# Two weight tiles side by side behind two normalizations, with filler matmuls moved into TensorE's idle times

## The chip, the cores and the metric

One core of a Trainium2 chip runs the whole program in one launch. The metric is the device time in microseconds (us), a median of several executions. The engines are named as in the profile: PE is TensorE (PEld its weight loads), DVE is VectorE, ACT is ScalarE, POOL is GpSimd, SP issues the DMAs.

## The reference

Two model blocks run one behind the other on one sequence of 1024 tokens with 1024 features, all in float32. Only the parts around the change are written out:

```python
# first block: two layers with an adaptive norm
for layer in range(2):
    shift, scale, gate = split(silu(c) @ ada_w[layer] + ada_b[layer], 3)
    h = rms_norm(x, norm_w[layer]) * (1 + scale) + shift
    y = even_mixer(h, ...) if layer % 2 == 0 else odd_mixer(h, ...)   # attention, gates, output projection
    x = x + gate * y
x = rms_norm(x, final_norm)

# odd_mixer: h @ w_in gives q (1024), k (256), v (256), gates (1024); windowed attention with a sink;
#            (attention * silu(gates)) @ w_out

# second block
h = rms_norm(x, norm1)
p = h @ w_in              # 512 lru_x, 512 lru_g, 256 q, 256 k, 512 v, 512 g, 16 z
lru = rg_lru(causal_conv(lru_x), ...) * gelu(lru_g)
gla = rms_norm(gated_linear_attention(q, k, v, z)) * silu(g)
x = x + concat(lru, gla) @ w_out
h = rms_norm(x, norm2)
gate, up = split(h @ w_ffn_in, 2)
x = x + (silu(gate) * up) @ w_ffn_out
return rms_norm(x, final_norm_2)
```

## The kernel before

**Layout.** Activations lie with features on the partitions: eight blocks of 128 features ("k" or "f") by 1024 tokens. A float32 product is made from a high part and a low part of each operand: the weight tile is `WH + WL`, the normalized activations are `HH + HL`, and a product is `HH*WH + HL*WH + HH*WL`.

**A weight tile.** Projections go through a list of tiles of 128 output features, numbered through the whole kernel. For tile `t`, SP loads the raw weights (`sp_weights`, it waits for `w_low` of tile `t - 2`), ACT rounds them to the high part (`act_high`, L241), POOL subtracts for the low part (`pool_low`, L246), PE makes 48 matmuls of 512 columns (`pe_tile`, L259: eight features of six matmuls each), and ACT or DVE takes the result out of PSUM (`act_evict`, L268, or `dve_residual`, L410). Tiles alternate between two places for the weights and two pairs of PSUM banks by `t % 2`. A tile can have places of its own (`own_places`); the first tile of each of the two output projections has them.

**A change of stage.** Between an output projection and the next projection stands the norm of `x`. ACT squares each feature block of the new `x` and DVE adds them up. PE sums over features with a column of ones (`pe_token_sums`, L348). ACT and DVE make the inverse root (L353, L358), DVE copies it out over 128 columns (`dve_spread`, L362), and PE turns it round into PSUM banks 6 and 7 (`pe_spread`, L368). Then the norm is applied feature by feature: DVE scales (L381), ACT adds the shift and rounds to `HH` (L392), DVE subtracts for `HL` (L386, which reads two operands in SBUF). The first tile of the projection is multiplied while this goes on: before its feature `k` PE waits for `n_low(n, k)`, which is `HL` of feature `k`. The second tile comes behind it in `pe_tile`'s order.

**Fillers.** `pe_stay_awake(n, bank)` (L343) issues `n` matmuls of 128 columns whose results nobody reads. Each gives two records in the profile.

**The three places.** `n = 1` is layer 1 of the first block: output projection `EVEN_OUT`, then the tiles `ODD_PROJ`. `n = 2` is the second block: output projection `ODD_OUT`, then `S_PROJ`. Here the spread is made twice: once for `final_norm` (it is copied to SBUF, L1863) and once, called "gained", for both norms in a row. `n = 3` is the norm before the feed-forward part, where DVE L2422 and L2433 and ACT L2428 take the place of L381, L386 and L392.

**Orders written by hand.** Each engine runs its own list of functions (`pe_...`, `act_...`), in program order. ACT makes the high part of tile `t + 1` before it takes out tile `t`. In `act_odd_proj` and `act_second_proj` the high part of the first tile comes before the normalization and that of the second tile behind it. SP issues all DMAs from one list: in `sp_odd_proj` the first tile's weights, then a 4 MB copy of `x` to memory (`spill`) that waits for the last residual, then the other tiles; in `sp_second_proj` the first tile's weights, then the recurrent weights `BD` and `WAL` that wait for DVE's memsets, then the others. `dve_conv(0)` needs tile 0 of `S_PROJ`; `pe_recurrent(0)`, behind feature 4 of tile 2, needs that convolution.

Of the kernel before, what the change touches and what calls it, by code (L numbers as in the profile page):

```python
# [14 lines left out]
P = 128  # L15
# [3 lines left out]
DT = DM // P  # L19
# [112 lines left out]
def build(nc, d, where, known):  # L132
# [71 lines left out]
    tiles = []  # L204
# [31 lines left out]
    def act_high(t):  # L236
        raw, high, _ = places(t)
        act.wait_ge(*w_loaded[t % 2].at(t))
        if t >= 2:
            act.wait_ge(*w_used.at(t - 2))  # L240
        act.activation(high[:, :, :], raw[:, :, :], ACT.Copy).then_inc(*w_high.up(t))  # L241
# [5 lines left out]

    def pe_tile(t, high, low, made=None, beside=None):
        s, w = t % 2, tiles[t]
        _, wh, wl = places(t)  # L250
        pe.wait_ge(*w_low.at(t))
        if t >= 2:
            pe.wait_ge(*evicted(t - 2))
        for k in range(w.kt):
            if made:
                pe.wait_ge(*made(k))
            for n, (wt, x) in enumerate(((wh, high), (wh, low), (wl, high))):
                for h in range(2):
                    last = pe.matmul(ps[0:w.m, 2 * s + h, :], wt[:, k, :], x[:, k, halves(h)],  # L259
                                     start=(k == 0 and n == 0), stop=(k == w.kt - 1 and n == 2))  # L260
            if k == w.kt - 1:
                last.then_inc(*w_used.up(t))
            if beside:
                beside(k)

    def act_evict(t, dst, func=ACT.Copy, scale=1.0):
# [31 lines left out]
    EVEN_OUT = [tile(cols(d["even_w_out"][0], i * P), gone="dve", own=None if i else EVEN_FIRST) for i in range(8)]  # L298
    ODD_KV = [tile(cols(odd_in, O_K + i * P)) for i in range(4)]
    ODD_Q = [tile(cols(odd_in, O_Q + i * P)) for i in range(8)]  # L300
    ODD_GATES = [tile(cols(odd_in, O_G + i * P)) for i in range(8)]
    ODD_OUT = [tile(cols(d["odd_w_out"][0], i * P), gone="dve", own=None if i else ODD_FIRST) for i in range(8)]
    S_LRU = [tile(cols(second_in, S_LX + i * P)) for i in range(4)]
    S_Z16 = tile(cols(second_in, S_Z + 16 - P))
# [5 lines left out]

    def act_tiles(ts, evict, first=False, upto=None):

        if first:
            act_high(ts[0])
        for i, t in enumerate(ts):
            if upto is None or t + 1 <= upto:
                act_high(t + 1)
            evict(i, t)

# [1022 lines left out]
    def pe_even_out():  # L1342
        pe.wait_ge(*e_done.at("B", N - 1))
        pe_stay_awake(14, 2 * (EVEN_OUT[0] % 2))
        for f, t in enumerate(EVEN_OUT):
            pe_tile(t, HH, HL, made=(lambda k: m_low.at(0, k)) if f == 0 else None)
        pe_stay_awake(12, 4)
        pe_token_sums(1, 4)
        pe_spread(1)
        pe_stay_awake(14, 0)  # L1350

# [39 lines left out]
    def sp_odd_proj():  # L1391
        sp_weights(ODD_PROJ[0])
        sp.wait_ge(*ev_dve.at(EVEN_OUT[-1]))
        sp.dma_start(d["spill"], X[:, :, :]).then_inc(*x_spilled.landed(1))
        for i, t in enumerate(ODD_PROJ[1:]):
            sp_weights(t)
            if i == 2:
                sp.dma_start(AWAY[:, :], const("away")).then_inc(*c_tables.landed(0))
                sp.dma_start(SLOPE[:, :], const("slopes")).then_inc(*c_tables.landed(1))
                sp.dma_start(SINK[:, :], d["c_sink"][0:1, :].to_broadcast([P, C_HEADS])).then_inc(*c_tables.landed(2))  # L1400

    def pe_odd_proj():
        for i, t in enumerate(ODD_PROJ):
            pe_tile(t, HH, HL, made=(lambda k: n_low.at(1, k)) if i == 0 else None)
            if 4 <= i < 6:
                f = i - 4
                pe.wait_ge(*ev_act.at(ODD_KV[2 + f]))
                for t in range(TT):
                    last = pe.transpose(pair(4 + 2 * f)[:, rows(t)], VFC[:, f, rows(t)], IDENT[:, :])
                last.then_inc(*vc_turned.up(f))  # L1410

    def act_odd_proj():
        act_high(ODD_PROJ[0])
        act_normalize(1, MOD[:, 24:32])
# [19 lines left out]

        act_tiles(ODD_PROJ, evict, upto=ODD_PROJ[-1])

# [372 lines left out]

    def pe_odd_out():  # L1810
        pe.wait_ge(*c_added.at(NG - 1))
        pe_stay_awake(15, 2 * (ODD_OUT[0] % 2))
        for f, t in enumerate(ODD_OUT):
# [87 lines left out]
    def sp_second_proj():  # L1901
        for j, t in enumerate(S_PROJ):
            sp_weights(t)
            if j == 0:
                sp.wait_ge(*bd_clear.at())
# [84 lines left out]
    def pe_second_proj():  # L1990
# [18 lines left out]

        for j, t in enumerate(S_PROJ):  # L2010
            pe_tile(t, HH, HL, made=(lambda k: n_low.at(2, k)) if j == 0 else None, beside=lambda k: beside(j, k))

# [56 lines left out]
    def act_second_proj():  # L2069
        act_high(S_PROJ[0])  # L2070
        act_normalize(2, None)
        for j, t in enumerate(S_PROJ):
            act_high(t + 1)
            if j in (3, 5, 7, 9):
# [198 lines left out]
    def pe_second_out():  # L2273
        for f, t in enumerate(S_OUT):
            pe_tile(t, HM, LM, made=(lambda k: m_low.at(2, k)) if f == 0 else None)
        pe_stay_awake(12, 4)
        pe_token_sums(3, 4, LAST.sq)
        pe_spread(3, LAST)
        pe_stay_awake(13, 0)
# [654 lines left out]
```

## Time and profile before

| | |
|---|---|
| median of 3 runs | 2529.44 us (2526.62 to 2530.26) |
| the profiled execution's own time | 2526.05 us |
| its span in the trace | 2524.7 us |
| mean granted clock of PE | 0.984 |
| PE busy | 2389.8 us, 95% |
| DVE, ACT, POOL busy | 1410.3, 1134.7, 918.5 us |

The granted clock is 1.00 at 2.4 GHz and 0.50 at 1.2 GHz. In the views of the trace, idle time stands in square brackets with what ended it; start times are from the span's start. Busy time is the union of an engine's records, so overlapping records count once.

### The profile page before, as it was taken

Reading aid. Unit: us, or ns where it says so; the run is one execution under the profiler, and the core shown is the slowest. Engines: PE = TensorE matmul, PEld = TensorE weight load, DVE = VectorE, ACT = ScalarE, POOL = GpSimd, SP = SyncE. Lnnn points to the kernel's source line nnn. Section 1 sums busy time; section 2 is a strip of 40 time slices with the busy share of each in tenths; the row PEclk is TensorE's granted clock in tenths of the full one; section 3 lists DMA queues with packets and bytes.
Section 4 is the critical chain, followed back from the end, with each engine's and each line's share of the span. In section 5 each row is a group of like instructions: output and inputs, shape, how many; then the busy total and the mean of one; then the engine's idle time right before and its main releaser. Section 6 shows DMA issues by size and latency. Waiting matters only on the chain.

```text
span 2524.7 us, 31336 instructions
## 1 busy us (share of the span) xinstructions
PE 2389.8 (95%) x12088; PEld 1955.3 (77%) x12088; DVE 1410.3 (56%) x1948; ACT 1134.7 (45%) x1753; POOL 918.5 (36%) x671
## 2 busy tenths in 40 slices
PE   4999999989999999999999999999989999999998
PEld 3778788868888778876678677788867888788876
DVE  5256499858884420149954743332556666665665
ACT  4322388778883221259942473231333333333334
POOL 0121234236642122335421211112265555566651
PEclk8999999999999999999999999999999999999999
DMA  8234300000003211100030411013201111111111
GB/s 293 73 117 135 106 6 1 1 18 1 1 1 117 100 54 49 43 1 1 10 117 22 133 34 42 26 29 113 67 26 51 50 51 50 51 50 51 50 57 69
DMA packets 152488, 143.23 MB, mean 57 GB/s; under 512 B 10358, under 2 KB 140692, under 8 KB 150420
## 3 DMA queue, kind: packets, MB, share of 16 engines
q1 hardware_dynamic: 152340, 141.22, 17.7%
q8 instruction: 97, 1.59, 0.3%
q14 instruction: 51, 0.42, 0.1%
HBM read 124.43 MB, written 16.78 MB: 56 GB/s over the span
## 4 chain that ended last, share of the span: by engine, by line
PE 66%; ACT 8%; DVE 8%; POOL 8%; issue 6%; DMA 4%; SPq 1%; ACTq 0%; DVEq 0%; POOLq 0%
PE ps L259 36%; PE ps L2509 6%; PE ps L1031 4%; POOL WSR L2398 4%; PE ps L2496 4%; PE ps L1054 3%; DMA WS<-in_w_ffn_in 3%; PE ps L1041 3%; POOL WSL L2416 2%; PE ps L2472 2%; ACT C_PR L1687 1%; DVE XF L2724 1%; POOL OWL L2640 1%; PE ps L1576 1%; ACT B_PR L1114 1%
## 5 line engine op out<-in xcount | busy, mean ns | idle before, releaser
L246 POOL TENSOR_TENSOR WL<-WR,WH 128x1024 fp32r<-128x1024 f32 (+1 forms) x91 | 211.3, 2322 | 909.5 <-ACT WH L241 909.4
L259 PE MATMUL ps<-HH,WH 128*128 128x512 f32 (+1 forms) x1168 | 374.8, 402 | 15.6 <-DVE HL L386 9.9
L259 PE MATMUL ps<-HL,WH 128*128 128x512 f32 (+1 forms) x1168 | 363.8, 393 | 0.0
L259 PE MATMUL ps<-HH,WL 128*128 128x512 f32 (+1 forms) x1168 | 363.0, 392 | 0.0
L259 PEld LDWEIGHTS ps<-HH,WH 128*128 128x128 f32 (+1 forms) x1168 | 214.7, 189 | 75.0 <-DVE HL L386 14.0
L259 PEld LDWEIGHTS ps<-HH,WL 128*128 128x128 f32 (+1 forms) x1168 | 220.1, 188 | 48.8
L259 PEld LDWEIGHTS ps<-HL,WH 128*128 128x128 f32 (+1 forms) x1168 | 219.8, 188 | 48.9
L2724 DVE TENSOR_TENSOR XF<-ps,XF 128x1024 f32<-128x1024 f32 x168 | 199.8, 1218 | 24.4 <-PE ps L2509 20.1
L2496 PE MATMUL ps<-HC,WSH 128*128 128x512 f32 x640 | 197.4, 390 | 4.8 <-DVE HC L2455 4.8
L2410 ACT ACTIVATE WSH<-WSR 128x512 fp32r<-128x512 f32 x100 | 63.2, 632 | 303.6 <-POOL WSR L2398 303.5
L2398 POOL TENSOR_TENSOR WSR<-WS 128x512 f32<-128x512 f32 x100 | 137.9, 1379 | 151.3 <-PE ps L2496 71.8
L1067 DVE TENSOR_REDUCE NM<-ps 128x1 f32<-128x1024 f32 x128 | 156.1, 1220 | 35.1 <-PE ps L1031 34.4
L2416 POOL TENSOR_TENSOR WSL<-WSR,WSH 128x512 fp32r<-128x512 f32 x100 | 135.3, 1353 | 79.1 <-ACT WSH L2410 79.1
L2496 PE MATMUL ps<-HS,WSH 128*128 128x512 f32 x480 | 149.1, 392 | 3.3 <-DVE HS L2455 3.3
L2496 PEld LDWEIGHTS ps<-HC,WSH 128*128 128x128 f32 x640 | 119.9, 188 | 30.8 <-DVE HC L2455 3.3
L2509 PE MATMUL ps<-AH,OWH 128*128 128x512 f32 x352 | 114.4, 406 | 11.0 <-DVE XF L2724 10.6
L2496 PE MATMUL ps<-HC,WSL 128*128 128x512 f32 x320 | 124.5, 389 | 0.0
L2684 DVE TENSOR_TENSOR CG<-CG,ps 128x512 f32<-128x512 f32 x60 | 41.3, 688 | 146.5 <-ACT CU L2570 94.0
L2509 PE MATMUL ps<-AH,OWL 128*128 128x512 f32 x352 | 109.9, 393 | 0.0
L2509 PE MATMUL ps<-AL,OWH 128*128 128x512 f32 x352 | 109.1, 391 | 0.0
L2496 PEld LDWEIGHTS ps<-HS,WSH 128*128 128x128 f32 x480 | 90.7, 189 | 22.9 <-issue 3.4
L1606 DVE CUSTOM_DVE_ANT_0 C_SB<-ps,BF,NSINK 128x384 f32<-128x384 f32 (+1 forms) x128 | 68.9, 576 | 69.4 <-POOL C_VS L1728 60.3
(411 smaller groups left out, 5160.7 us busy)
## 6 DMA issues: line engine op xcount, KB each, us to landing
WS<-in_w_ffn_in SPq DMA_DIRECT2D x44, 512.0 KB, 5.0
MKW<-in_ada_w SPq DMA_DIRECT2D x32, 512.0 KB, 4.2
spill<-X SPq DMA_DIRECT2D x3, 4096.0 KB, 13.2
OW<-in_w_ffn_out SPq DMA_DIRECT2D x22, 512.0 KB, 3.4
WR<-in_w_in SPq DMA_DIRECT2D x21, 512.0 KB, 3.7
WR<-in_odd_w_in SPq DMA_DIRECT2D x20, 512.0 KB, 3.6
WR<-in_even_w_in SPq DMA_DIRECT2D x17, 512.0 KB, 4.9
AWK<-in_ada_w SPq DMA_DIRECT2D x8, 1024.0 KB, 10.1
```

Source lines behind the costliest of these rows:

```text
L246: pool.tensor_tensor(low[:, :, :], raw[:, :, :], high[:, :, :].bitcast(F32), ALU.subtract).then_inc(*w_low.up(t))
L259: last = pe.matmul(ps[0:w.m, 2 * s + h, :], wt[:, k, :], x[:, k, halves(h)], start=(k == 0 and n == 0), stop=(k == w.kt - 1 and n == 2))
L1031: last = pe.matmul(ps[:, b + j, :], qs[:, rows(q)], ks[:, halves(j)], start=(n == 0), stop=(n == len(passes) - 1))
L1041: last = pe.transpose(ps[:, 4 + j, rows(k)], D.PR[:, p % 3, rows(4 * j + k)], IDENT[:, :])
L1054: last = pe.matmul(ps[:, 6 + pg % 2, 0:2 * P], D.VS[D.v_of(h)][:, k, :], pt[pg % 2][:, k, :], start=(k == 0 and n == 0), stop=(k == TT - 1 ...
L1067: dve.tensor_reduce(NM[:, s % 4:s % 4 + 1], pair(2 * (s % 2)), AX_X, ALU.max, negate=True).then_inc(*m_done.up(g, s))
L1606: dve.tensor_tensor_reduce(C_SB[:, hd, WIN - w:WIN], ps[:, j, 0:w], BF[i % 2][:, hd, b0:b0 + w], -1.0, NSINK[:, 4 * i + hd:4 * i + hd + 1] ...
L2398: pool.tensor_tensor(WSR[:, q % RING, :, :], w_block(*a), w_block(*b), op).then_inc(*ws_sum.up(q))
L2416: pool.tensor_tensor(WSL[:, q % RING, :, :], src, WSH[:, q % RING, :, :].bitcast(F32), ALU.subtract).then_inc(*ws_low.up(q))
L2496: last = pe.matmul(ps[:, BANK[o], :], w[:, q % RING, k, :], OPERAND[o][:, x, k, :], start=(k == 0 and n == 0), stop=(k == HK - 1 and n == 2))
L2509: done = pe.matmul(ps[:, 4 + 2 * (n % 2) + h, :], w[:, rows(n)], x[:, halves(h)], start=(first and m == 0), stop=(last and m == 2))
L2724: dve.tensor_tensor(LAST.x[:, n, :], pair(4 + 2 * (n % 2)), LAST.x[:, n, :], ALU.add).then_inc(*y_added.up(r, n))
```

## The change

Both first tiles get their weights early and are multiplied in turn, feature by feature, for six features; then the first tile's last two features, then the second's. For that the first tile of each of the two projections has places of its own (`KEYS_FIRST`, `LRU_FIRST`), ACT makes both high parts before the normalization, SP issues three (layer 1) or two (second block) tiles' weights before the DMAs named above, and `act_high` waits for the last user of the shared place. The fillers are set differently at three stage changes: five more before the spreads `n = 1` and `n = 3` (and 13 in place of 14 behind the first of these); at the start of `ODD_OUT` seven stand before the wait for the attention's last result and nine behind it, where 15 stood behind it.

```diff
 def act_high(t):
+        user = t - 2
+        while user >= 0 and tiles[user].own:
+            user -= 2
         act.wait_ge(*w_loaded[t % 2].at(t))
-        if t >= 2:
-            act.wait_ge(*w_used.at(t - 2))
+        if user >= 0:
+            act.wait_ge(*w_used.at(user))

+    def pe_feature(t, k, high, low):        # the six matmuls of one feature, with pe_tile's waits at k == 0
+        ...
+    def pe_two_tiles(first, second, high, low, made):
+        for k in range(DT - 2):
+            pe.wait_ge(*made(k))
+            pe_feature(first, k, high, low)
+            pe_feature(second, k, high, low)
+        for t in (first, second):
+            for k in range(DT - 2, DT):
+                pe.wait_ge(*made(k))
+                pe_feature(t, k, high, low)

+    KEYS_FIRST, LRU_FIRST = own_places("KEYS_FIRST", 59, 63, 67), own_places("LRU_FIRST", 67.25, 71.25, 75.25)
-    ODD_KV = [tile(cols(odd_in, O_K + i * P)) for i in range(4)]
+    ODD_KV = [tile(cols(odd_in, O_K + i * P), own=None if i else KEYS_FIRST) for i in range(4)]
-    S_LRU = [tile(cols(second_in, S_LX + i * P)) for i in range(4)]
+    S_LRU = [tile(cols(second_in, S_LX + i * P), own=None if i else LRU_FIRST) for i in range(4)]

+    def act_two_tiles(first):
+        act_high(first)
+        act_high(first + 1)

 def pe_even_out():
         pe_token_sums(1, 4)
+        pe_stay_awake(5, 5)
         pe_spread(1)
-        pe_stay_awake(14, 0)
+        pe_stay_awake(13, 0)

 def sp_odd_proj():
-        sp_weights(ODD_PROJ[0])
+        for t in ODD_PROJ[:3]:
+            sp_weights(t)
         sp.wait_ge(*ev_dve.at(EVEN_OUT[-1]))
         sp.dma_start(d["spill"], X[:, :, :]).then_inc(*x_spilled.landed(1))
-        for i, t in enumerate(ODD_PROJ[1:]):
+        for i, t in enumerate(ODD_PROJ[3:]):
             sp_weights(t)
-            if i == 2:
+            if i == 0:
                 ...

 def pe_odd_proj():
+        pe_two_tiles(ODD_PROJ[0], ODD_PROJ[1], HH, HL, lambda k: n_low.at(1, k))
         for i, t in enumerate(ODD_PROJ):
-            pe_tile(t, HH, HL, made=(lambda k: n_low.at(1, k)) if i == 0 else None)
+            if i >= 2:
+                pe_tile(t, HH, HL)

 def act_odd_proj():
-        act_high(ODD_PROJ[0])
+        act_two_tiles(ODD_PROJ[0])
         act_normalize(1, MOD[:, 24:32])
         ...
-        act_tiles(ODD_PROJ, evict, upto=ODD_PROJ[-1])
+        act_high(ODD_PROJ[2])
+        evict(0, ODD_PROJ[0])
+        evict(1, ODD_PROJ[1])
+        for i, t in enumerate(ODD_PROJ):
+            if i >= 2:
+                if i + 1 < len(ODD_PROJ):
+                    act_high(t + 1)
+                evict(i, t)

 def pe_odd_out():
+        pe_stay_awake(7, 0)
         pe.wait_ge(*c_added.at(NG - 1))
-        pe_stay_awake(15, 2 * (ODD_OUT[0] % 2))
+        pe_stay_awake(9, 2 * (ODD_OUT[0] % 2))

 def sp_second_proj():
         for j, t in enumerate(S_PROJ):
             sp_weights(t)
-            if j == 0:
+            if j == 1:
                 sp.wait_ge(*bd_clear.at())

 def pe_second_proj():
-        for j, t in enumerate(S_PROJ):
-            pe_tile(t, HH, HL, made=(lambda k: n_low.at(2, k)) if j == 0 else None, beside=lambda k: beside(j, k))
+        pe_two_tiles(S_PROJ[0], S_PROJ[1], HH, HL, lambda k: n_low.at(2, k))
+        for j, t in enumerate(S_PROJ[2:], 2):
+            pe_tile(t, HH, HL, beside=lambda k: beside(j, k))

 def act_second_proj():
-        act_high(S_PROJ[0])
+        act_two_tiles(S_PROJ[0])
         act_normalize(2, None)
         for j, t in enumerate(S_PROJ):
-            act_high(t + 1)
+            if j == 0:
+                act_high(t + 2)
+            elif j > 1:
+                act_high(t + 1)

 def pe_second_out():
         pe_token_sums(3, 4, LAST.sq)
+        pe_stay_awake(5, 5)
         pe_spread(3, LAST)
```

## Rows read from the trace of the kernel before

**Rows 1.** Page, part 1: busy us, share, instructions by engine.
```profile
PE 2389.8 (95%) x12088; PEld 1955.3 (77%) x12088; DVE 1410.3 (56%) x1948; ACT 1134.7 (45%) x1753; POOL 918.5 (36%) x671
```

**Rows 2.** Waits of PE, whole span: us in total, times, longest.
```profile
PE ps L259 <- DVE HL L386: 9.9, 12, 0.9
PE ps L259 <- POOL WL L246: 7.2, 6, 1.9
```

**Rows 3.** Timeline, layer 1's first tiles: start, us, instructions, [idle before].
```profile
871.04 0.71 PE L259 MATMUL ps<-HH,WH 128*128 128x512 f32 x2
...
875.13 0.74 PE L259 MATMUL ps<-HH,WH 128*128 128x512 f32 x2 [0.86 <-DVE HL L386]
...
890.16 0.84 PE L259 MATMUL ps<-HH,WH 128*128 128x512 f32 x2 [1.94 <-POOL WL L246]
...
902.78 0.62 PE L259 MATMUL ps<-HH,WH 128*128 128x512 f32 x2
```

**Rows 4.** Windows: length, busy (records) of the five engines, PE clock, DMA, GB/s.
```profile
888.20:890.60 2.40, 0.46 (x3) 0.40 (x3) 2.33 (x3) 1.97 (x2) 2.20 (x2) 1.00 0.00 0
...
1275.00:1276.50 1.50, 0.00 (x0) 0.00 (x0) 0.83 (x2) 0.59 (x1) 0.00 (x0) 0.95 0.00 0
1276.50:1279.80 3.30, 3.26 (x15) 3.26 (x16) 1.32 (x2) 2.48 (x3) 0.72 (x1) 0.51 0.38 112
...
863.30:866.90 3.60, 2.65 (x13) 2.65 (x14) 1.50 (x3) 0.88 (x1) 2.36 (x1) 0.50 0.98 414
866.90:870.10 3.20, 3.20 (x17) 3.20 (x17) 3.14 (x4) 2.30 (x2) 0.00 (x0) 0.50 0.76 199
```

**Rows 5.** Timeline, stage change into layer 1.
```profile
860.84 1.95 PE L348 MATMUL ps<-ONEC,SQX 128*128 128x1 f32 x16 [1.05 <-DVE SQX L338]
...
864.25 1.97 PE L368 MATMUL ps<-IDENT,SQX 128*128 128x128 f32 x8 [1.47 <-DVE SQX L362]
864.26 2.36 POOL L246 TENSOR_TENSOR WL<-WR,WH 128x1024 fp32r<-128x1024 f32 x1 [22.98 <-ACT WH L241]
...
866.26 2.47 DVE L381 SCALAR_TENSOR_TENSOR T<-X,GS,ps 128x1024 f32<-128x1024 f32 x2 [2.06 <-PE ps L368]
...
868.76 1.28 DVE L386 SCALAR_TENSOR_TENSOR HL<-T,MOD,HH 128x1024 fp32r<-128x1024 f32 x1
```

**Rows 6.** Timeline, start of the output projection ODD_OUT.
```profile
1276.54 5.13 PE L343 MATMUL ps<-IDENT 128*128 128x128 f32 x30 [1.56 <-DVE C_O L1644]
...
1278.48 4.63 DVE L406 TENSOR_TENSOR HL<-MIX,HH 128x1024 fp32r<-128x1024 f32 x4 [1.99 <-ACT HH L401]
...
1281.43 0.70 PE L259 MATMUL ps<-HH,ODD_FIRST 128*128 128x512 f32 x2
```

**Rows 7.** Timeline, stage change into the second block and its first two tiles.
```profile
1376.78 2.48 PE L343 MATMUL ps<-IDENT 128*128 128x128 f32 x10
...
1379.47 2.36 POOL L246 TENSOR_TENSOR WL<-WR,WH 128x1024 fp32r<-128x1024 f32 x1 [25.40 <-ACT WH L241]
...
1382.52 0.69 DVE L362 COPY SQX<-RC 128x1024 f32<-128x1024 f32 x1
...
1384.15 2.98 PEld L343 LDWEIGHTS ps<-IDENT 128*128 128x128 f32 x26
...
1388.26 0.70 PE L259 MATMUL ps<-HH,WH 128*128 128x512 f32 x2 [0.94 <-DVE HL L386]
...
1406.32 0.73 PE L259 MATMUL ps<-HH,WH 128*128 128x512 f32 x2 [0.44 <-POOL WL L246]
...
1417.34 0.62 PE L259 MATMUL ps<-HH,WH 128*128 128x512 f32 x2
```

**Rows 8.** Timeline, DVE and POOL at the same time, second block.
```profile
1409.22 3.31 DVE L2137 SCALAR_TENSOR_TENSOR CV<-LX,COLB,CV 128x1024 f32<-128x1024 f32 x1
...
1407.97 3.47 POOL L246 TENSOR_TENSOR WL<-WR,WH 128x1024 fp32r<-128x1024 f32 x1 [1.70 <-ACT WH L241]
```

**Rows 9.** DVE's conv instructions, L2137: ns min/median/max.
```profile
L2137 DVE SCALAR_TENSOR_TENSOR CV<-LX,COLB,CV x12: 1283/1285/3306, 1407.9 to 1496.0; 128x1024 f32<-128x1024 f32 x12
```

**Rows 10.** Timeline, spread before the feed-forward part.
```profile
1796.22 1.97 PE L368 MATMUL ps<-IDENT,SQF 128*128 128x128 f32 x8 [1.47 <-DVE SQF L362]
```

**Rows 11.** Windows, late in the second projection.
```profile
1600.00:1620.00 20.00, 20.00 (x98) 16.87 (x98) 4.93 (x4) 4.85 (x5) 2.44 (x1) 0.74 0.10 27
```

## What the change will do, predicted before it was run

> **What bounds the kernel now.** I read the page first: PE is busy for 2389.8 of 2524.7 us [rows 1], so what can be won is the some 135 us in which it idles, and time in which it runs at half clock. The waits of PE come next. Of its waits inside the tiles' matmuls (L259), the two largest are 9.9 us for `HL` in 12 pieces and 7.2 us for `WL` in six [rows 2]. The timeline shows where they lie. In layer 1 the first tile starts at 871.04, and before a feature PE idles some 0.86 us [rows 3], because DVE delivers a feature each 2.5 us (two instructions of 1.24 to 1.28 us, [rows 5]) and six matmuls need less. Then the second tile waits 1.94 us for its low weights, since ACT made their high part only behind the normalization. Tile 2 starts at 902.78 [rows 3]. In the second block tile 0 starts at 1388.26, tile 1 at 1406.32, tile 2 at 1417.34 [rows 7]. The windows show the clock: 1.00 up to 890.6 with PE almost idle from 888.2 [rows 4]. The matmuls from 890.16 on then run partly at half clock: the tile takes 902.78 - 890.16 = 12.6 us, and the one at full clock in the second block 1417.34 - 1406.32 = 11.0 us.
>
> **Two tiles in turn, layer 1.** Removed: the waits per feature, the wait for `WL`, and the 1.6 us of half clock. A pair of features costs PE 2 x 11.0 / 8 = 2.75 us, more than DVE's 2.5, so after the first feature PE never waits: `HL` of feature 7 is there at most 7 x 2.51 = 17.6 us after that of feature 0, and PE asks for it behind 13 features' work, 17.9 us after its start. Both tiles take 22.0 us from PE's start. Switching tile and bank at each feature I cost at nothing: two tiles behind each other also switch and show no gap (902.78). Bounded from above by the 0.86 us of a real wait, 12 switches would cost 10 us; nothing speaks for it, as nothing is waited for.
>
> PE's start: five fillers now stand before the spread. The sums end at 862.8 and the spread began at 864.25 [rows 5]. Ten records take 2.48 us at half clock [rows 7] and some 1.2 us at full (26 records of the fillers from 1384.15 took 2.98, [rows 7]). The clock fell at 863.3 [rows 4], so they take about 2.0 us: the spread starts at 864.9, 0.6 later than now, and DVE behind it too. `HL` of feature 0 was ready at 868.76 + 1.28 = 870.04, and now at 870.7. In return PE has no gap in front of the spread. Where it was busy without a gap from the fall on, the clock was back after 3.3 us (1276.5 to 1279.8, [rows 4]); with the gap it was low up to 870.1 [rows 4]. So it should be back at 866.7, 13 fillers take 3.1 us, and PE starts at 870.7 with `HL`, against 871.04. Were the clock low to 870.1 after all, it would start at 871.7. Tile 2 then starts at 870.7 + 22.0 = 892.7: **10.1 us won**, between 9.1 and 10.4.
>
> What could be late next. POOL makes the second low part at 866.6 to 869.0, directly behind the first (2.36 us from 864.26, [rows 5]), and DVE's first L386 comes at 869.4: no meeting. If they met, it would cost what is left of POOL's instruction, at most 2.4 us. Tile 2's high part comes behind the normalization (about 887.2), its low part is ready at 891, its banks are free at about 891, and PE comes at 892.7: cover of 1.7 us. The spill now waits behind the weights of tile 2, which wait for POOL at 866.6: about 8 us later; only the eviction of tile 4, 20 us behind 892.7, waits for it. ACT's second high part (1.04 us) lies in ACT's idle time before the first `T`. From tile 2 on all is paced by PE and moves forward as a whole.
>
> **Fillers at the start of ODD_OUT.** PE idles 1.5 us before 1276.5, the clock falls, and 30 filler records take 5.13 us, so the first tile starts at 1281.43 although its first `HL` is ready at 1278.48 + 1.16 = 1279.7 [rows 4, 6]. Seven fillers in the idle time (1.6 us at full clock) keep PE busy, and nine behind the wait take 2.1 us at full clock. The tile then starts at 1279.75: 1.7 us won. If the clock falls anyway, the nine take 4.4 us and 0.3 us is won. I take **1.6**.
>
> **Two tiles, second block.** By the same sum tile 2 would start at 1388.26 + 22.0 = 1410.3, against 1417.34: 7.1 us. But here the second low part meets something. POOL's first ran from 1379.47 to 1381.83 [rows 7], and now the second follows to 1384.2. DVE's copy for the spread "gained" started at 1382.52 and took 0.69 us [rows 7]; in front of it is a tiny instruction with two operands in SBUF. Such a meeting is in the trace: while POOL ran from 1407.97 to 1411.44, DVE's L2137 took 3.31 us [rows 8], where its kind takes 1.285 [rows 9]; it ended one normal length after POOL did. So both DVE instructions wait for 1384.2, and the copy ends near 1385.1 instead of 1383.2: 1.9 us on the path of the spread. By itself this costs between 0 (if a copy of one operand is not held) and 2.3 us. The Trainium skill (SBUF — State Buffer, "Who interferes with whom") says that VectorE and GpSimd share one port pair as an exclusive lock, that a copy in a 2-port mode and any VectorE instruction with two SBUF inputs need it, and that the later one waits for the whole instruction. By that rule the copy is held as I have it; the rows show it for two-input instructions, and here it speaks against making both weights early.
>
> PE meanwhile has nothing from 1382.6 to 1385.1, 2.5 us. A gap of 1.9 us was followed by half clock [rows 4], so I expect the clock to fall here. The spread (8 records, 1.97 us low against 1.0) and the 26 filler records (2.98 at full, some 6.4 all low) then end at 1391 to 1393.5; with no fall, `HL` at 1390.1 sets the start. I take 1391.4, 3.1 us later than before: **4.0 us won**, between 1.9 and 7.1. Downstream: conv(0) ends some 6 us after tile 0 and `pe_recurrent(0)` is asked for 6.8 us after tile 1, so it is covered.
>
> **Five fillers before the feed-forward part.** The spread began at 1796.22 after an idle 1.47 us [rows 10], the same pattern: 0.6 us later, clock earlier. Nothing lies behind it that gains. I take **0**, between 0.9 lost and 0.3 won.
>
> **Sum.** 10.1 + 1.6 + 4.0 + 0 = 15.7 us. The profiled execution took 2526.05 us (span 2524.7 and 1.35 around it) and would take 2510.4. It was 3.4 us quicker than the median of 2529.44. On the median: 2513.7.
>
> **Rivals.**
> - A, no price in the second block: the copy isn't held by POOL, or the clock stays up. Then the second block wins 5.3 to 7.1 us, for a sum of about 18 and 2511.4. For it: the L1863 copy next door reads PSUM and may be of the kind that isn't held. Against it: [rows 8].
> - B, the gain of the second block is used up: the low-clock fillers run to 1393.5 and a wait of DVE's chain (conv(0), then eight updates of X, then recurrence 0) reaches PE. Then only 11.7 us remain: 2517.7. Against it: DVE's end of the updates has some 3 us of cover before recurrence 0.
> - C, the other side: the clock. Late in the second projection PE was busy for all of 20 us at a mean clock of 0.74 [rows 11], so half of that stretch ran low and lost 5 us. Which stretches are caught changes when everything moves by 12 to 16 us. A microsecond at half clock loses half a microsecond, so 21 us more of it than now would eat 10.7 of the 15.7 us and leave less than 0.2% (5 us); 31 us would eat all. The likely size is 7 us either way (3.5 us of time), for a time of 2517 or 2510; 2525 or more needs three or four such stretches together.
> - D, the change doesn't do what it says: PE waits at each switch, up to 0.86 us a time; 24 switches lose 20 us, for 2534. Against it: nothing releases PE there.
>
> **How the numbers follow.** Chances: forecast 0.52, A 0.22, B 0.15, C at its deciding size 0.07, D 0.04. The bounds of the terms, all bad at once, give 9.1 + 0.3 + 1.9 - 0.9 = 10.4 us, and all good 10.4 + 1.7 + 7.1 + 0.3 = 19.5: 2519.0 to 2509.9. C's usual 3.5 us either way, which rarely meets either end in full, makes it 2506 to 2521. About 5 us, 0.2%, is what a measurement of this kernel can tell from no change. Faster: all of the forecast, A and B, and part of C: 0.93. Same: the rest of C and part of D, 0.04. Slower: 0.03.
>
> **What the profile after would show.** Right: no waits of L259 for `HL` behind the first feature in layer 1; tile 2 of `ODD_PROJ` 22 us after the first matmul; the first tile of `ODD_OUT` some 3.2 us behind the wait for the attention, with the clock at 1.00; a copy L362 of more than 2 us or a tiny L1864 of 1.8 us beside a POOL L246 in the second block. Wrong: that copy at 0.69 us in time (A); idle PE in tile 2 of `S_PROJ` (B); a mean clock far below 0.984 (C); gaps inside the pairs (D). The whole prediction fails if a stage behind the tiles isn't paced by PE and waits for something that hasn't moved, for which I see only the spill.

## The result and the profile after

| | before | after |
|---|---|---|
| median of 4 runs | 2529.85 us | 2511.43 us (2508.98 to 2513.62) |
| ratio | 1 | 0.9934, 95% interval 0.9918 to 0.995 |
| span of the profiled execution | 2524.7 us | 2510.5 us |
| mean granted clock of PE | 0.984 | 0.983 |

2513.7 us was predicted, with 2506 to 2521 around it. A second measurement of the same kernel, told below, gave 2511.62 us and a ratio of 0.9919 (0.9899 to 0.994).

In kernel.py of the changed kernel the lines have moved: the matmuls of a tile are L260, the high and low parts L244 and L249, the fillers L358, the sums L363, the copy for the spread and the spread L377 and L383, the two normalization instructions L396 and L401, the residual L425, evictions L286, the split of the mix L421.

**Layer 1.** The timeline of the changed kernel answers to [rows 3, 5]. The execution was 3.0 us late when it came here (the last residual of EVEN_OUT starts at 860.15, before at 857.16), behind code that differs only in how its lines are grouped, so positions are counted from that residual. The first line is of the kernel before, the others are of the changed one:

```profile
857.16 1.28 DVE L410 SCALAR_TENSOR_TENSOR X<-ps,MOD,X 128x1024 f32<-128x1024 f32 x1 [7.24 <-PE ps L259]
...
860.15 1.28 DVE L425 SCALAR_TENSOR_TENSOR X<-ps,MOD,X 128x1024 f32<-128x1024 f32 x1 [7.24 <-PE ps L260]
...
863.84 2.51 PE L363 MATMUL ps<-ONEC,SQX 128*128 128x1 f32 x16 [1.05 <-DVE SQX L353]
866.21 2.48 PE L358 MATMUL ps<-IDENT 128*128 128x128 f32 x10
868.49 1.91 PE L383 MATMUL ps<-IDENT,SQX 128*128 128x128 f32 x8
870.19 3.87 PE L358 MATMUL ps<-IDENT 128*128 128x128 f32 x26
874.28 0.72 PE L260 MATMUL ps<-HH,KEYS_FIRST 128*128 128x512 f32 x2 [0.22 <-DVE HL L401]
...
875.77 0.62 PE L260 MATMUL ps<-HH,WH 128*128 128x512 f32 x2
...
877.15 0.62 PE L260 MATMUL ps<-HH,KEYS_FIRST 128*128 128x512 f32 x2
...
896.19 0.62 PE L260 MATMUL ps<-HH,WH 128*128 128x512 f32 x2
```

The five fillers stand between sums and spread, and the spread begins 8.34 us behind the residual in place of 7.09. `KEYS_FIRST` (tile 0) and `WH` (tile 1) take turns, one feature each, with no idle time in square brackets behind the first. Tile 2 starts at 896.19, which is 21.9 us behind the start of tile 0 and 36.0 us behind the residual. Before it was 902.78 - 857.16 = 45.6: 9.6 us won. PE's waits between 872 and 897 are one:

```profile
PE ps L260 <- DVE HL L401: 0.2, 1, 0.2
```

**ODD_OUT.** 32 filler records now start right behind the attention's last product, in place of 30 after a wait [rows 6], and the windows show the clock at 1.00 on both sides of it, where it was 0.51 [rows 4]:

```profile
1268.08 4.00 PE L358 MATMUL ps<-IDENT 128*128 128x128 f32 x32
1268.91 0.85 DVE L1670 TENSOR_TENSOR C_O<-ps,C_OT 64x256 f32<-64x256 f32 x2 [1.52 <-ACT C_OT L1725]
...
1273.03 0.73 PE L260 MATMUL ps<-HH,ODD_FIRST 128*128 128x512 f32 x2 [0.94 <-DVE HL L421]
```

```profile
1264.90:1268.10 3.20, 1.76 (x10) 1.25 (x9) 1.74 (x4) 0.59 (x1) 0.88 (x2) 1.00 0.00 0
1268.10:1273.10 5.00, 4.05 (x34) 3.67 (x32) 2.18 (x4) 3.10 (x4) 0.72 (x1) 1.00 0.21 60
```

The attention's last additions start at 1268.91 here and the tile 4.12 us behind them. In the kernel before, the additions are these, and the tile started 5.79 us behind them:

```profile
1275.64 0.85 DVE L1644 TENSOR_TENSOR C_O<-ps,C_OT 64x256 f32<-64x256 f32 x2 [1.51 <-ACT C_OT L1699]
```

**Second block.** The same stretch as [rows 7], ahead of it the last residual of ODD_OUT:

```profile
1360.40 1.28 DVE L425 SCALAR_TENSOR_TENSOR X<-ps,MOD,X 128x1024 f32<-128x1024 f32 x1 [6.11 <-PE ps L260]
...
1371.20 2.36 POOL L249 TENSOR_TENSOR LRU_FIRST<-LRU_FIRST,LRU_FIRST 128x1024 fp32r<-128x1024 f32 x1 [25.53 <-ACT LRU_FIRST L244]
1373.51 2.34 POOL L249 TENSOR_TENSOR WL<-WR,WH 128x1024 fp32r<-128x1024 f32 x1
...
1374.17 1.71 DVE L1891 TENSOR_TENSOR GAINS<-COLA 128x8 f32<-128x8 f32 x1
1375.80 0.68 DVE L377 COPY SQX<-RC 128x1024 f32<-128x1024 f32 x1
...
1376.63 1.56 PE L383 MATMUL ps<-IDENT,SQX 128*128 128x128 f32 x8 [2.38 <-DVE SQX L377]
1377.98 4.25 PE L358 MATMUL ps<-IDENT 128*128 128x128 f32 x26
1381.99 0.71 PE L260 MATMUL ps<-HH,LRU_FIRST 128*128 128x512 f32 x2
```

L1891 (L1864 in the kernel before) multiplies two vectors of eight columns, both in SBUF. It started 0.66 us after POOL's second subtraction and ended with it, at 1375.88 after 1375.85. The copy behind it is its normal length but late, and PE idles 2.38 us in front of the spread. The windows show what the clock does about that gap: it falls behind it, and the fillers run partly low.

```profile
1374.00:1376.00 2.00, 0.25 (x3) 0.06 (x1) 2.00 (x3) 0.00 (x0) 1.85 (x1) 1.00 0.00 0
1376.00:1378.00 2.00, 1.37 (x9) 1.41 (x10) 1.69 (x5) 0.00 (x0) 0.00 (x0) 0.76 0.00 0
1378.00:1380.00 2.00, 2.00 (x11) 2.00 (x11) 1.77 (x2) 0.46 (x1) 0.00 (x0) 0.50 0.24 55
```

The second tile is taken out at 1404.06, which is 43.7 us behind the last residual of ODD_OUT (1360.40). Before it was 1417.54 behind 1368.80, or 48.7: 5.1 us won. The last two lines are of the kernel before.

```profile
1404.06 1.03 ACT L286 ACTIVATE LX<-ps 128x1024 f32<-128x1024 f32 x1 [1.69 <-PE ps L260]
...
1368.80 1.28 DVE L410 SCALAR_TENSOR_TENSOR X<-ps,MOD,X 128x1024 f32<-128x1024 f32 x1 [6.11 <-PE ps L259]
1417.54 1.03 ACT L268 ACTIVATE LX<-ps 128x1024 f32<-128x1024 f32 x1 [9.64 <-PE ps L259]
```

### The profile page after: what moved, and what is told of

It is laid out like the page before. It is cut to its first block, busy times and chain, and to the rows that moved or that the text cites. A ratio compares the mean times of both kernels' runs of the same rounds, so it can differ in the third digit from the quotient of the medians.

```text
span 2510.5 us, 31376 instructions
## 1 busy us (share of the span) xinstructions
PE 2388.4 (95%) x12108; PEld 1959.3 (78%) x12108; DVE 1407.2 (56%) x1948; ACT 1136.6 (45%) x1753; POOL 919.9 (37%) x671
## 4 chain that ended last, share of the span: by engine, by line
PE 66%; ACT 9%; POOL 7%; DVE 7%; issue 6%; DMA 4%; SPq 1%; ACTq 0%; DVEq 0%; POOLq 0%
PE ps L260 37%; PE ps L2541 6%; PE ps L1046 4%; POOL WSR L2430 4%; PE ps L2528 4%; PE ps L1069 3%; DMA WS<-in_w_ffn_in 3%; PE ps L1056 3%; POOL WSL L2448 2%; PE ps L2504 2%; ACT C_PR L1713 1%; DVE XF L2756 1%; POOL OWL L2672 1%; ACT B_PR L1129 1%; ACT B_PTH L1123 1%
## 5 line engine op out<-in xcount | busy, mean ns | idle before, releaser
L249 POOL TENSOR_TENSOR WL<-WR,WH 128x1024 fp32r<-128x1024 f32 (+1 forms) x89 | 208.4, 2342 | 843.7 <-ACT WH L244 843.5
L260 PE MATMUL ps<-HH,WH 128*128 128x512 f32 (+1 forms) x1136 | 361.9, 400 | 3.1 <-POOL WL L249 1.7
L260 PE MATMUL ps<-HL,WH 128*128 128x512 f32 (+1 forms) x1136 | 352.4, 391 | 0.0
L260 PE MATMUL ps<-HH,WL 128*128 128x512 f32 (+1 forms) x1136 | 351.7, 391 | 0.0
L260 PEld LDWEIGHTS ps<-HH,WH 128*128 128x128 f32 (+1 forms) x1136 | 209.1, 188 | 56.1 <-issue 10.1
L260 PEld LDWEIGHTS ps<-HL,WH 128*128 128x128 f32 (+1 forms) x1136 | 213.1, 188 | 47.2
L260 PEld LDWEIGHTS ps<-HH,WL 128*128 128x128 f32 (+1 forms) x1136 | 213.1, 188 | 47.0
## 6 DMA issues: line engine op xcount, KB each, us to landing
spill<-X SPq DMA_DIRECT2D x3, 4096.0 KB, 13.6
```

The costliest lines, as they stand in the source:

```text
L249: pool.tensor_tensor(low[:, :, :], raw[:, :, :], high[:, :, :].bitcast(F32), ALU.subtract).then_inc(*w_low.up(t))
```

## The experiments

One table serves them all. It has one profile of each run; e5, e6 and e7 were timed only once. Each profile is cut at the same marks, by start times in the timeline. *Start-up*: to the last residual of EVEN_OUT. *Layer 1*: from there to ACT's eviction of the second tile (0.2 us behind the start of tile 2). *Attention*: to the start of the attention's last additions. *ODD_OUT*: to its first matmul. *Copy*: from the last residual of ODD_OUT to the copy "gained". *Second*: from that residual to the eviction of the second tile. *Rest 2*: from there to the last residual of S_OUT, with the mean clock of the window. *FF*: from there to the first matmul of the feed-forward part. *Held*: how long the tiny instruction took.

| kernel | start-up | layer 1 | attention | ODD_OUT | copy | second | rest 2, clock | FF | held |
|---|---|---|---|---|---|---|---|---|---|
| before | 857.2 | 45.8 | 372.7 | 5.79 | 13.7 | 48.7 | 371.6, 0.98 | 13.5 | 0.16 |
| changed | 860.2 | 36.2 | 372.5 | 4.12 | 15.4 | 43.7 | 370.1, 0.98 | 13.1 | 1.71 |
| changed, again (e10) | 861.9 | 35.3 | 371.3 | 4.13 | 16.1 | 45.5 | 368.5, 0.99 | 14.1 | 2.01 |
| e1 layer 1 only | 858.4 | 35.8 | 372.4 | 4.27 | 13.6 | 48.7 | 371.6, 0.98 | 13.6 | 0.16 |
| e2 second block only | 864.6 | 44.5 | 372.8 | 5.90 | 15.1 | 43.4 | 371.6, 0.98 | 13.4 | 1.72 |
| e3 fillers only | 861.6 | 45.8 | 372.8 | 4.13 | 15.0 | 50.0 | 366.8, 0.99 | 14.1 | 0.16 |
| e4 second high late | 866.8 | 35.4 | 371.3 | 4.13 | 14.2 | 41.9 | 368.4, 0.99 | 14.1 | 0.16 |
| e5 no spread fillers | 865.3 | 35.7 | 372.7 | 4.12 | 14.6 | 44.0 | 368.4, 0.99 | 13.4 | 2.06 |
| e6 gap filled | 865.4 | 35.4 | 372.5 | 4.13 | 14.6 | 42.9 | 366.8, 0.99 | 12.0 | 1.74 |
| e7 15 behind the wait | 861.8 | 35.0 | 370.4 | 7.20 | 17.0 | 45.3 | 370.2, 0.98 | 13.1 | 1.72 |
| e8 both highs early | 867.5 | 35.3 | 372.6 | 4.12 | 12.9 | 40.6 | 368.5, 0.99 | 13.8 | 0.16 |
| the same again (e11) | 857.3 | 35.3 | 372.7 | 4.12 | 15.3 | 43.1 | 366.8, 0.99 | 12.0 | 0.16 |
| e9 early, not in turn | 862.1 | 42.0 | 370.5 | 4.12 | 14.6 | 49.7 | 371.8, 0.98 | 12.8 | 1.92 |

### e1: the tiles in turn in layer 1 alone

`pe_second_proj`, `act_second_proj`, `sp_second_proj`, `LRU_FIRST` and all fillers as before; layer 1 as in the changed kernel.

> Two tiles in turn in layer 1 alone, all else as before. Theory: the 9.6 us that the changed kernel wins between the last residual of EVEN_OUT and tile 2 of ODD_PROJ come from the tiles in turn, not from the fillers: tile 2 starts 45.6 - 10 = 35 to 36 us behind that residual, no wait of L260 for HL behind the first feature, ratio 0.996 (about 2519.5 for 2529.5). Rival (the fillers and the clock are what won): tile 2 at 40 us or later, ratio 0.998 or nearer to 1.

Measured: 2523.83 us, ratio 0.9969 (0.9956 to 0.9981). Layer 1 takes 35.8 us without any filler moved, so the 10 us are the tiles'. In the medians it is less, 7.0 us; the 0.996 that was expected lies in the interval. Unexpected: ODD_OUT took 4.27 us although its fillers were the old ones; the clock hadn't fallen there this time.

### e2: the tiles in turn in the second block alone

> Two tiles in turn in the second block alone. Theory: tile 2 of S_PROJ comes 43 to 44 us behind the last residual of ODD_OUT (48.5 before), with DVE's tiny L1891-kind instruction and the copy behind it held by POOL's second subtraction (1.7 us in place of 0.16), ratio 0.998. Rival (the lock came only from the way the rest had moved): the copy isn't held and tile 2 comes at 41.5 us, ratio 0.997.

Measured: 2527.21 us, ratio 0.9981 (0.9968 to 0.9994). The hold is there (1.72 us), the copy starts 15.1 us in, and the second block takes 43.4 us. The hold belongs to making both weights early at this place, not to how the rest had moved.

### e3: the fillers alone

> Only the fillers are moved. Theory: the first tile of ODD_OUT starts 4.1 us behind the start of the attention's last addition in place of 5.8 (1.7 us won); the five fillers in front of the spreads win nothing, within 0.5 us either way; ratio 0.9993. Rival (keeping TensorE awake is worth as much as the tiles in turn): ratio 0.997 or less.

Measured: 2528.47 us, ratio 0.999 (0.9978 to 1.0001): not told from no change. ODD_OUT shows its 1.7 us. The second block, whose code here is that of before, took 1.3 us more and "rest 2" 4.8 us less, both without a cause in the code. The clock is what differs: it was low during the sums here, which took 2.31 and 3.55 us (before 1.95 and 2.62), and the copy came 1.3 us later; in "rest 2" its mean was 0.99, not 0.98.

### e4: the second high part behind the copy

```diff
 def act_second_proj():
-        act_two_tiles(S_PROJ[0])
+        act_high(S_PROJ[0])
+        act.wait_ge(*spread_made.at("gained"))
+        act_high(S_PROJ[1])
```

> The changed kernel, but in the second block ACT makes the second tile's high part only when the copy for the spread is done, so POOL's second subtraction can't hold DVE. Theory: the tiny DVE instruction is back at 0.17 us, TensorE's gap in front of the second spread shrinks from 2.4 to about 0.7 us, tile 2 of S_PROJ comes 41.3 us behind the last residual of ODD_OUT (43.5 in the changed kernel), 2.2 us less in all. Rival 1: POOL's instruction now meets the first HL (two SBUF operands) and holds it, tile 2 at 43 us again. Rival 2: the clock, not the hold, sets TensorE's start, tile 2 at 43 us with DVE early.

Measured: 2512.49 us, ratio 0.993 (0.9913 to 0.9946). The tiny instruction is back at 0.16 us and the second block at 41.9 us: 1.7 us less than the changed kernel (2.2 expected), and neither rival came. Rival 1 missed by little: POOL's subtraction ended 0.1 us before DVE's first `HL` started. In the whole time e4 and the changed kernel (ratios 0.9934 and 0.9919) can't be told apart.

```profile
1379.06 0.16 DVE L1891 TENSOR_TENSOR GAINS<-COLA 128x8 f32<-128x8 f32 x1
1379.13 0.69 DVE L377 COPY SQX<-RC 128x1024 f32<-128x1024 f32 x1
...
1379.96 1.06 PE L383 MATMUL ps<-IDENT,SQX 128*128 128x128 f32 x8 [1.19 <-DVE SQX L377]
1380.86 3.07 PE L358 MATMUL ps<-IDENT 128*128 128x128 f32 x26
1384.78 0.73 PE L260 MATMUL ps<-HH,LRU_FIRST 128*128 128x512 f32 x2 [0.85 <-DVE HL L401]
```

The gap is 1.19 us, the clock stays up (26 records in 3.07 us), and PE waits for `HL`, not for its own fillers.

### e5: without the fillers in front of the spreads

`pe_stay_awake(5, 5)` out of `pe_even_out` and `pe_second_out`, 14 fillers behind the first spread again.

> The changed kernel without the five fillers in front of the spreads of layer 1 and of the feed-forward part. Theory: they are worth nothing that stays: the first tile of layer 1 comes 13.6 to 13.9 us behind the last residual (14.1 with them), tile 2 follows 21.8 us later as before, the feed-forward part starts 13.4 to 13.6 us behind its last residual (13.1 with them). Rival: without them the clock stays low into the tiles in turn and tile 2 of layer 1 comes a microsecond or more later.

Measured once, 2516.91 us: layer 1 35.7 us, FF 13.4, all as expected. So in time and in segments the five fillers are worth too little to be told by this pair. All profiles together say more. With them layer 1's first matmul comes 12.9 to 14.1 us behind the residual (nine profiles, eight of them at 12.9 to 13.3), without them 13.6 to 13.9 (four). The clock says why: in each of the four profiles without them it stood at 0.50 for 6.8 us at this place, in the eight for only 3.4 us. The changed kernel's first profile is the ninth; there it was low for 6.8 us too. The first two lines are of e1, without the fillers, the last two of e10, with them:

```profile
863.10:866.50 3.40, 1.94 (x10) 1.85 (x10) 1.06 (x3) 1.45 (x3) 0.22 (x1) 0.50 0.02 5
866.50:869.90 3.40, 3.40 (x17) 3.40 (x17) 1.62 (x2) 0.96 (x2) 3.40 (x2) 0.50 0.02 6
...
867.40:870.80 3.40, 3.40 (x18) 3.40 (x18) 1.06 (x3) 2.10 (x3) 1.74 (x1) 0.50 0.00 0
870.80:874.20 3.40, 3.39 (x30) 3.19 (x29) 2.85 (x3) 1.52 (x2) 2.95 (x2) 1.00 0.29 74
```

### e6: the gap in the second block filled

```diff
 def pe_odd_out():
         pe_spread(2)
-        pe_stay_awake(4, 0)
+        pe_stay_awake(13, 0)
         pe.wait_ge(*scale_copied.at())
```

> The changed kernel with 13 in place of 4 fillers behind the first spread of the second block, so that TensorE has no gap while DVE's copy is held. Theory: the hold by POOL is 1.7 us of the loss and stays (the tiny instruction still takes some 1.7 us), the clock is worth at most 0.5 us: tile 2 of S_PROJ 43.0 to 43.6 us behind the last residual of ODD_OUT. Rival (the clock that falls behind the gap is most of the loss): tile 2 at 42.2 us or less.

Measured once, 2510.19 us. The second block took 42.9 us, between the two expectations, and the table says why that is no gain of the fillers: the copy already started 0.8 us earlier (14.6 to 15.4), ahead of the place that was changed. From the copy's start to the eviction it is 28.3 us in both. Behind the fillers the clock was up (the spread took 1.04 us, in the changed kernel 1.56), but they ended 0.7 us after the copy and so delayed the spread:

```profile
1379.32 0.68 DVE L377 COPY SQX<-RC 128x1024 f32<-128x1024 f32 x1
...
1380.73 1.04 PE L383 MATMUL ps<-IDENT,SQX 128*128 128x128 f32 x8
```

What the clock's fall costs is told better by the profiles with an unfilled gap. There are six (changed, e10, e2, e5, e7, e9), and in all six the clock fell in it or right behind it; in the seven others it didn't fall there. From the copy's start to the first matmul it is 5.6 to 5.7 us where it didn't fall (e6, held up by its own fillers, 6.2), 6.2 where it was low for 3.4 us (changed, e2, e7), and 7.3 to 7.4 where it was low for 6.8 us (e10, e5, e9). So the fall costs 0.5 us in three and 1.6 to 1.8 us in three.

### e7: all fillers of ODD_OUT behind the wait again

> The changed kernel with the 15 fillers of ODD_OUT all behind the wait again. From the kernels so far: with 7 + 9 the first tile starts 4.12 us behind the start of the attention's last addition in every one, with 15 behind the wait 5.8 and 5.9 in two and 4.3 in one, whose work lay otherwise to the clock's falls. Theory: what the new setting gives is that the clock never falls in the gap; this kernel shows 4.3 if the clock happens to stay and 5.8 to 5.9 if it falls before the tile, and the granted clock of that stretch says which. Rival: the fillers in front of the wait save their own time (15 take 3.1 us less than the 5 us, whatever the clock), then 5.8 with the clock at 1.00.

Measured once, 2514.47 us: 7.20 us, outside both theories. The clock stood at 0.51 for all of the 15 fillers, 6.54 us of them:

```profile
1268.16 6.54 PE L358 MATMUL ps<-IDENT 128*128 128x128 f32 x30 [1.57 <-DVE C_O L1670]
1274.46 0.71 PE L260 MATMUL ps<-HH,ODD_FIRST 128*128 128x512 f32 x2
```

```profile
1268.10:1274.40 6.30, 6.24 (x29) 6.24 (x30) 4.30 (x5) 5.45 (x6) 0.73 (x1) 0.51 0.78 281
```

So the old setting gave 4.27, 5.79, 5.90 and 7.20 us in four profiles, and the new one 4.12 or 4.13 in nine of nine, with the clock at 1.00.

### e8 and e11: both high parts before the root

```diff
 def act_odd_out():
         def gained(f):
             act_square("gained", f, SQG, ...)
+            if f == 6:
+                act_high(S_PROJ[0])
         act_out_tiles(ODD_OUT, 2, gained)
+        act_high(S_PROJ[1])
         act_root(2)
 def act_second_proj():
-        act_two_tiles(S_PROJ[0])
```

> The changed kernel, but in the second block ACT makes the first tile's high part during ODD_OUT and the second's before the root, so that both of POOL's subtractions are over before DVE starts on the norm. Theory: no DVE instruction is held, the copy starts 13.7 us behind the last residual of ODD_OUT as in the kernel before (15.4 in the changed one), tile 2 of S_PROJ comes at 41.5 us or a little less (43.7 by ACT's eviction in the changed one). In total 2 us better than the changed kernel, which a ratio can't tell apart surely. Rival: ACT's work moved in front of the root delays the root and takes the gain back.

Measured: 2506.83 us, ratio 0.9906 (0.9889 to 0.9922). POOL is done with both parts before DVE starts on the root, nothing is held, the copy starts 12.9 us in and the second block takes 40.6 us.

```profile
1360.43 2.58 POOL L249 TENSOR_TENSOR LRU_FIRST<-LRU_FIRST,LRU_FIRST 128x1024 fp32r<-128x1024 f32 x1 [8.30 <-ACT LRU_FIRST L244]
1371.30 2.53 POOL L249 TENSOR_TENSOR WL<-WR,WH 128x1024 fp32r<-128x1024 f32 x1 [8.29 <-ACT WH L244]
```

It was run again beside the changed kernel, on the same chip:

> The changed kernel, unaltered, once more beside the next one. Ratio 0.9925 to 0.994. Its second profile shows how much of the segments is chance: layer 1 35.3 to 36.3 us, ODD_OUT 4.12, second block 43 to 44 us by the eviction, and the time from there to the last residual of the second block 366 to 372, by how much low clock falls into it.

> The kernel with the second block's high parts made before the root, once more on the same chip as the changed kernel. Theory: 2 to 3 us (0.1%) below the changed kernel's median, ratio to before 0.991 to 0.993; second block 40.6 to 41.6 us by the eviction. Rival: the two can't be told apart in time although the segment is shorter.

Measured: the changed kernel 2511.62 us, ratio 0.9919 (0.9899 to 0.994); this one 2509.59 us, ratio 0.9912 (0.9889 to 0.9936). Both medians favour it, by 4.6 (in separate measurements) and 2.0 us, and the intervals overlap: the whole isn't told apart. Nor did the segments come out as expected: the changed kernel's second block took 45.5 us, with 43 to 44 expected, and this one's 43.1, with 40.6 to 41.6 expected. That lies inside the 42.9 to 45.5 of the six profiles in turn with the hold, so the segment as a whole doesn't tell them apart either. What does is that nothing is held, and the stretch from the copy on. The same code took 40.6 us in one profile and 43.1 in the other because of the sums: 16 + 16 records of L363 took 1.95 and 1.93 us in e8, and in e11

```profile
1360.52 2.64 PE L363 MATMUL ps<-ONEC,SQX 128*128 128x1 f32 x16 [1.05 <-DVE SQX L353]
1363.02 3.55 PE L363 MATMUL ps<-ONEC,SQG 128*128 128x1 f32 x16
```

The clock had fallen in the midst of the first. From the copy's start to the eviction the two agree (27.8 us each, and 27.7 in e4); with the hold it is 28.2 to 29.4.

### e9: weights early, but one tile behind the other

```diff
     def pe_two_tiles(first, second, high, low, made):
-        for k in range(DT - 2):
-            ...
         for t in (first, second):
-            for k in range(DT - 2, DT):
+            for k in range(DT):
```

> The changed kernel with both weights made early as there, but the two tiles one behind the other. Theory: in layer 1 only the wait for WL (1.9 us) and the half clock behind it (1.6 us) are won, tile 2 by the eviction 42.3 us behind the last residual of EVEN_OUT (45.8 before, 36.2 in turn); in the second block 0.5 us of WL wait is won and 1.9 us lost to the hold, tile 2 no earlier than the 48.7 of before. Ratio 0.998. Rival (early weights are most of the gain): layer 1 at 38 us or less.

Measured: 2523.24 us, ratio 0.9975 (0.9961 to 0.999). Layer 1 42.0 us, second block 49.7, both as expected. PE waits for `HL` in front of seven features of the first tile, six times for 0.85 to 0.87 us, and one of these is (L397 is L401 of the other kernels)

```profile
877.56 0.73 PE L260 MATMUL ps<-HH,KEYS_FIRST 128*128 128x512 f32 x2 [0.85 <-DVE HL L397]
```

So of the roughly 10 us in layer 1, 3.8 come with the early weights and 6 to 7 with taking turns. Part of the 3.8 is PE's start, which moves with the clock (13.0 us behind the residual in e9, 13.9 in before). Counted from PE's first matmul to the eviction, it is 31.9 us in before (30.9 and 32.9 in e2 and e3, which have the old order), 29.0 in e9 and 22.1 in turn: 2.9 us for the early weights, 6.9 for the turns.

In the second block the same count gives 29.3 us in before and 27.7 in e9, so the early weights win 1.6 us there too; but PE starts 2.6 us later, behind the hold and the low clock. The 49.7 us in sum is no loss that one profile can show, since the old order took 48.7, 48.7 and 50.0: there the early weights alone win nothing.

## Why the prediction was right

- **Two tiles in turn, layer 1: 10.1 predicted, 9.6 in the profile, 9.6 to 10.8 over the nine profiles that have them, against the 45.8 of before (the old order took 44.5 and 45.8 in e2 and e3).** The mechanism was right in each part: a pair of features costs PE more than DVE needs, 21.9 us from start to tile 2 (22.0 predicted), no cost for switching tiles (no gap inside the pairs of either stage, in any profile that has them: rival D is out), a clock at 1.00 over the tiles. e1 shows it belongs to this part of the change, e9 splits it.
- **PE's start in layer 1: 870.7 against 871.04 was predicted, 0.35 us earlier; it was 0.25 later in the profiled execution.** The step that was off took the clock's fall for fixed. It fell during the sums this time (they took 2.51 us, 1.95 before), so all ten filler records ran low (2.48 us, not 2.0), and the spread came 1.25 us later, not 0.6. Nor was the clock back after 3.3 us: it stayed low for 6.8 us, as in before, and came back 11.7 us behind the residual in place of 13.0 only because it had fallen earlier. In the other eight profiles with the fillers it was low for 3.4 us, as the prediction has it, and PE started 0.6 to 0.9 us earlier than in before. So this part of the mechanism is right, and the profiled execution was the exception.
- **ODD_OUT: 1.6 predicted, 1.67 measured,** and in nine of nine profiles. e7 and e1 show that the old setting was a draw between 4.3 and 7.2 us.
- **Second block: 4.0 predicted, 5.1 measured.** The hold was right in its place, its cause and its size: the copy 1.9 us late predicted, 1.7 measured. L1891 took 1.71 us in the profile, 1.7 to 2.1 in the seven profiles that have the hold, 0.16 in the six that don't; e4 and e8 take it away by moving only ACT's high parts and with them POOL's work. It started 0.3 to 0.7 us behind POOL's subtraction and in all seven ended 0.02 to 0.03 us behind it: how long it took is how long POOL still had to go. The trace thus bears out for a two-input instruction the rule of the Trainium skill (SBUF — State Buffer, "Who interferes with whom"): the later instruction waits for the whole of the earlier one. For the copy itself nothing is shown, since L1891 stands in front of it and took the whole wait. (A tensor_scalar of 128x4 with one input in SBUF was held too: 2.31 us in place of 0.17, at 892.05 beside a subtraction from 891.94 on.) What was mis-sized is the second term, the clock behind the gap: PE was to start 3.1 us later, 1.9 of it for the hold and 1.2 for the clock, and started 2.1 us later. The clock did fall (0.76, then 0.50), but from the copy's start to the eviction that cost 28.3 - 27.8 = 0.5 us, because DVE's memset and first `T` and `HL` took most of that time anyway. That it was 0.5 and not the 1.6 to 1.8 of e10, e5 and e9 is luck; the 1.2 lies between.
- **Feed-forward part: 0 predicted, 0.4 won in the profile,** with 12.0 to 14.1 us in nine profiles with the fillers and 13.4 to 13.6 in four without. One profile of each can't tell that from nothing. Among the nine it goes with the clock: 12.0 where it didn't fall before the first matmul, 12.8 to 13.1 where it was low for 3.4 us, 13.8 to 14.1 where for 6.8.
- **Sum: 15.7 predicted, 9.6 + 1.7 + 5.1 + 0.4 = 16.8 in the profile's segments.** The spans differ by 14.2, since start-up took 3.0 us more, "rest 2" 1.6 less and the feed-forward part 1.3 more. The medians differ by 18.4, and by 21.8 in the second measurement. That the sum comes within 3 us of the first of these is partly luck: layer 1 fell 0.5 us short and the second block gave 1.1 more, and stretches that the change doesn't touch moved by as much as 10 us from profile to profile.
- **Rival C, the clock in stretches that the change doesn't touch,** is real, with a smaller size than its deciding one. Over 13 profiles "rest 2", whose code is in essence the same in all, took 370.1 to 371.8 us at a mean clock of 0.98 and 366.8 to 368.5 at 0.99. That is up to 5 us by chance, about as much as the second block gained.
- **Rival B** didn't come: PE has no wait at all between 1403 and 1710 in the changed kernel. **Rival A** didn't come in either form: the 1.71 us and the clock's fall are both there. (That POOL holds the copy as such is not shown.)

Parts and whole agree within their intervals: 0.9969 x 0.9981 x 0.999 = 0.994, and the changed kernel had 0.9934 and 0.9919.

## What to carry to other kernels

Where a producer delivers a piece each 2.5 us and the consumer needs 1.4 us for it, give the consumer two jobs on each piece: that won 6.9 us here, more than anything done to the wait between the jobs. Work that is made early "in idle time" must be looked at for what it shares: POOL's subtraction was in its own idle time, and held an eight-column DVE instruction on the critical path for 1.7 us; moved behind the copy or in front of the root it held nothing. Judge such a change by segments between marks of the timeline in several profiles, because the same code moves by up to 5 us a segment with the clock.

## What was not expected of the hardware

- The first 857 to 867 us of the program do the same work in all 13 kernels and spread over 10 us. Much of it goes with the same hold, in another place. Near 260 us DVE adds up a weight that a DMA has just brought (L492, two tensors in SBUF) at about the time at which POOL makes a low part, and the sums of PE wait for DVE. In five profiles (e2, e4, e5, e6, e8) POOL started 0.1 to 0.3 us before DVE: L492 took 3.1 to 3.4 us in place of 1.28, PE idled for 2.95 us, and the clock fell for 6.8 us. These are the five profiles with a start-up of 864.6 us and more. In the eight others DVE's instruction started first: L492 took 1.28 us, PE idled 0.7 us at most, and the start-up took 857.2 to 862.1. The lines are of e8:

```profile
261.75 2.35 POOL L249 TENSOR_TENSOR WL<-WR,WH 128x1024 fp32r<-128x1024 f32 x1 [7.64 <-ACT WH L244]
261.87 3.31 DVE L492 SCALAR_TENSOR_TENSOR MKA<-MKW,CS,MKA 128x1024 f32<-128x1024 f32 x1 [1.79 <-DMA MKW<-in_ada_w]
265.28 3.42 PE L503 MATMUL ps<-ONEC,MKA 128*128 128x1 f32 x16 [2.96 <-issue]
```

  The rest of the spread stays open.
- The clock's fall isn't tied to a place in the code. With the same 1.6 us of idle time in front of 30 filler records, they took 3.62 us (e1, clock 1.00), 5.13 (before) and 6.54 (e7, 0.51).
- Sums with one column leave PE busy by the records, and yet in the four profiles that are quoted here (before, changed, e8, e11) the clock fell during or just behind them: 16 records took 1.95 us where it fell behind them, 2.51 and 2.64 where it fell during them.
